# Gate, up and gated-unit projections: one 512-column matmul for the high weights in place of two of 256 columns

## The reference, cut to what matters

```
hidden = silu(h @ w_gate) * (h @ w_up)      # 11 chunks of 256 columns
x      = x + 0.5 * (hidden @ w_down)
```

## Time and profile before

| | |
|---|---|
| median of 3 runs | 1920.85 us (1920.28 to 1928.02) |
| the profiled execution's own time | 1923.98 us |
| its span, first to last instruction | 1922.2 us |
| mean granted TensorE clock | 0.972 of full speed |
| PE busy | 96% of the span |
| DVE busy | 43% |
| ACT busy | 34% |
| POOL busy | 9% |

### The profile page before, as it was taken

The page is one execution under the profiler, slowest core; times in us unless marked ns, Lnnn a source line. Parts: engine busy times, 40 slices in busy tenths (PEclk is TensorE's granted clock), DMA queues, the critical chain, the costliest instruction groups (busy, mean ns, idle before and its releaser), DMA issues.

```text
span 1922.2 us, 29735 instructions
## 1 busy us (share of the span) xinstructions
PE 1839.8 (96%) x12660; PEld 1520.6 (79%) x12660; DVE 835.5 (43%) x1028; ACT 652.4 (34%) x739; POOL 167.6 (9%) x83
## 2 busy tenths in 40 slices
PE   6997879999999998999999999999999999999998
PEld 4973744454554547999997999999999789999997
DVE  4325421111111107554576555565556445566544
ACT  3424210000000005434435543454435445354342
POOL 0110000000000000111000021112111000212110
PEclk8999879999999999999899999999999999999999
DMA  9329549999999995655543255555554545345550
GB/s 337 106 93 371 237 186 421 421 422 421 422 423 421 422 412 166 211 176 185 187 132 132 98 187 182 190 193 183 191 179 154 175 153 168 140 156 195 175 189 30
DMA packets 192020, 444.16 MB, mean 231 GB/s; under 512 B 9174, under 2 KB 140623, under 8 KB 164151
## 3 DMA queue, kind: packets, MB, share of 16 engines
q1 hardware_dynamic: 188736, 437.84, 61.7%
q10 hardware_dynamic: 2776, 2.90, 0.5%
q0 software_dynamic: 416, 2.09, 0.3%
HBM read 441.73 MB, written 1.06 MB: 230 GB/s over the span
## 4 chain that ended last, share of the span: by engine, by line
PE 92%; DVE 3%; ACT 2%; issue 1%; DMA 1%; ACTq 0%; POOL 0%; DVEq 0%
PE wk L1081 12%; PE wk L692 11%; PE wk L693 11%; PE wk L694 11%; PE acc L692 6%; PE acc L693 6%; PE acc L694 6%; PE wk L1101 6%; PE wk L1045 3%; PE acc L1061 3%; PE wk L742 2%; PE wk L743 2%; PE wk L745 1%; PE wk L770 1%; PE wk L778 1%
## 5 line engine op out<-in xcount | busy, mean ns | idle before, releaser
L522 DVE TENSOR_TENSOR w_lo<-ring,w_hi 128x2048 fp32r<-128x2048 f32 x197 | 452.0, 2297 | 391.9 <-ACT w_hi L513 391.8
L513 ACT ACTIVATE w_hi<-ring 128x2048 fp32r<-128x2048 f32 x198 | 377.4, 1907 | 510.5 <-PE wk L694 303.2
L692 PE MATMUL wk<-h_hi,w_hi 128*128 128x256 f32 x1752 | 499.0, 285 | 5.0 <-DVE h_lo L1951 5.0
L693 PE MATMUL wk<-h_lo,w_hi 128*128 128x256 f32 x1752 | 497.5, 284 | 0.0
L694 PE MATMUL wk<-h_hi,w_lo 128*128 128x256 f32 x1752 | 497.4, 284 | 0.0
L692 PEld LDWEIGHTS wk<-h_hi,w_hi 128*128 128x128 f32 x1752 | 338.2, 193 | 6.6 <-issue 6.5
L693 PEld LDWEIGHTS wk<-h_lo,w_hi 128*128 128x128 f32 x1752 | 338.1, 193 | 0.1
L694 PEld LDWEIGHTS wk<-h_hi,w_lo 128*128 128x128 f32 x1752 | 338.1, 193 | 0.0
L692 PE MATMUL acc<-hid_hi,w_hi 128*128 128x256 f32 x896 | 254.5, 284 | 2.7 <-POOL hid_lo L1838 2.7
L693 PE MATMUL acc<-hid_lo,w_hi 128*128 128x256 f32 x896 | 253.5, 283 | 0.0
L694 PE MATMUL acc<-hid_hi,w_lo 128*128 128x256 f32 x896 | 253.5, 283 | 0.0
(11 more groups left out here) (336 smaller groups left out, 2082.4 us busy)
## 6 DMA issues: line engine op xcount, KB each, us to landing
ring<-in_ffn_w_in_dram SPq DMA_DIRECT2D x88, 1024.0 KB, 5.1
ring<-in_w_gate_dram SPq DMA_DIRECT2D x64, 1024.0 KB, 13.7
ex_ring<-in_w_up_dram SPq DMA_DIRECT2D x64, 1024.0 KB, 17.0
ring<-in_ffn_w_out_dram SPq DMA_DIRECT2D x44, 1024.0 KB, 4.8
ex_ring<-in_w_down_dram SPq DMA_DIRECT2D x32, 1024.0 KB, 13.5
arena<-in_w_down_dram SPq DMA_DIRECT2D x32, 1024.0 KB, 12.6
ring<-in_w_ada_dram SPq DMA_DIRECT2D x24, 1024.0 KB, 7.8
ring<-in_b_w_in_dram SPq DMA_DIRECT2D x24, 1024.0 KB, 5.2
```

Source lines behind the costliest of these rows:

```text
L513: nc.scalar.activation(w_hi[:, v % SPLIT, 0:n], ring[:, u % RING, 0:n], ACT.Copy).then_inc(w_hi_ready, 1)
L522: eng.tensor_tensor(w_lo[:, v % SPLIT, 0:n], ring[:, u % RING, 0:n], w_hi[:, v % SPLIT, 0:n].bitcast(F32), ALU.subtract).then_inc(w_lo_rea ...
L692: mm(dst, w[0], x[0], start=first, stop=False, skip_group_check=True)
L693: mm(dst, w[0], x[1], start=False, stop=False, skip_group_check=True)
```

## The change

`h_hi` and `h_lo` become two halves of one tile `h_both`, so that one matmul can stream 256 high and 256 low columns (two runs, 2,048 elements apart). Its 512 results fill a whole bank: columns 0 to 255 hold high x high, columns 256 to 511 hold high x low, and a second matmul of 256 columns adds low weight x high activation to the latter. For each k-tile and m this is a 512-column and a 256-column matmul in place of three of 256 columns. The first gate unit of each layer keeps three matmuls of 256 columns (`first_halves_apart`).

A result takes two banks: gate always banks 0 and 1, up always 2 and 3, U units alternate between the pairs. The two column halves are added outside PE: ACT copies the low half to SBUF (`low_half`, `u_low_half`), DVE adds it to the high half (`summed`, and an add in `hidden` and in `scaled_u`), and then DVE does what it did before, from SBUF. The waits follow: gate and up of a chunk wait until the sums of the chunk before are made; a U unit waits for the sum two units earlier, and the first U unit for all results of the wide units. `totals` writes into an `acc` bank, and its wait is now ahead of the first down; `turn_wsp` writes into banks 0 and 1.

```diff
+        h_both = sb("h_both", [P, 2, KT, T], F32R)
+        h_hi, h_lo = h_both[:, 0, :, :], h_both[:, 1, :, :]
...
+            def halves_apart(banks, v):
+
+                wh, wl = halves(w_hi, v), halves(w_lo, v)
+                for m in range(2):
+                    f = slice(m * P, (m + 1) * P)
+                    for k in range(KT):
+                        mm(banks[:, m, :], wh[:, k, f], h_both[:, :, k, :], start=k == 0, stop=False,
+                           skip_group_check=True)
+                        last = mm(banks[:, m, T:2 * T], wl[:, k, f], h_hi[:, k, :], start=False, stop=k == KT - 1,
+                                  skip_group_check=True)
+                return last
...
 gate_up (PE)
-                            if i is not None:
-                                pe.wait_ge(hidden_ready, i * LOOP + (c0 + ch - 1))
...
-                        o = wk[:, 2 * (ch % 2) + j, :]
+                        if ch:
+                            n = c0 + ch
+                            pe.wait_ge((gate_summed, up_summed)[j], n if i is None else i * LOOP + n)
+                        banks = wk[:, 2 * j:2 * j + 2, :]
...
-                            last = project3(o, v)
+                            last = halves_apart(banks, v)
...
 U units (PE)
-            for a in range(12, 24):
-                v = split(U_B + a)
-                group(lambda b: project3(b, v), ends_unit=True)
+            pe.wait_ge(grp_out, g[0])
+            for a in range(12):
+                v = split(U_B + 12 + a)
+                if a >= 2:
+                    pe.wait_ge(u_summed, a - 1)
+                halves_apart(wk[:, 2 * (a % 2):2 * (a % 2) + 2, :], v).then_inc(unit_done, 1)
...
 swiglu (ACT)
+                    low_half(ch, i, 0)
                     split_high(v + SPLIT, i)
...
                     silu(ch, i)
+                    low_half(ch, i, 1)
                     split_high(v + 1 + SPLIT, i)
...
 swiglu (DVE), ahead of scaled, which now reads sil:
+                    dve.wait_ge(gate_copied, c0 + ch + 1 if i is None else i * LOOP + (c0 + ch + 1))
+                    V.tensor_tensor(sil[:, ch % 2, :, :], wk[:, 0:2, 0:T], gate_low, ALU.add).then_inc(gate_summed, 1)
...
 hidden (DVE)
+                    dve.wait_ge(up_copied, at(c0 + ch + 1))
+                    V.tensor_tensor(hid[:, ch % 2, :, :], wk[:, 2:4, 0:T], up_low, ALU.add).then_inc(up_summed, 1)
...
             for a in range(12):
+                u_low_half(a)
                 act.wait_ge(grp_out, 43 + 12 + a + 1)
...
 scaled_u (DVE)
+                dve.wait_ge(u_copied, a + 1)
+                b = wk[:, 2 * (a % 2):2 * (a % 2) + 2, :]
+                V.tensor_tensor(u_scaled_sb[:, a % 2, :, :], b[:, :, 0:T], u_low[:, a % 2, :, :], ALU.add).then_inc(u_summed, 1)
+                dve.wait_ge(u_summed, a + 1)
```

More of the change, by code:

```diff
@@ L283, in build @@
         sil_scaled = sem("sil_scaled")
+        gate_summed, up_summed, u_summed = sem("gate_summed"), sem("up_summed"), sem("u_summed")
+        gate_copied, up_copied, u_copied = sem("gate_copied"), sem("up_copied"), sem("u_copied")
         w_hi_ready, w_lo_ready, h_hi_ready, h_lo_ready = (sem("w_hi_ready"), sem("w_lo_ready"), sem("h_hi_ready"),
@@ L488, in build @@
         u_scaled_sb = nc.alloc_sbuf_tensor_at("u_scaled_sb", [P, 2, 2, T], F32, offset=hid_at)
+        u_low = nc.alloc_sbuf_tensor_at("u_low", [P, 2, 2, T], F32, offset=hid_at + 16 * T)
+        gate_low, up_low = (gated[:, 2048 + 512 * q:2560 + 512 * q].rearrange("p (m t) -> p m t", m=2) for q in range(2))
         def halves(hi, v, w=UW, rows=False):
@@ L712, in high_terms, with first_halves_apart @@
                 return mm(dst, w[1], x[0], start=False, stop=False, skip_group_check=True)
+            def halves_apart(banks, v):
[8 more added lines that the diff above has]
+                return last
+            def first_halves_apart(banks, v, fresh):
+                wh, wl = halves(w_hi, v), halves(w_lo, v)
+                for k in range(KT):
+                    pe.wait_ge(h_hi_ready, fresh + k + 1)
+                    for m in range(2):
+                        f = slice(m * P, (m + 1) * P)
+                        mm(banks[:, m, 0:T], wh[:, k, f], h_hi[:, k, :], start=k == 0, stop=False, skip_group_check=True)
+                        mm(banks[:, m, T:2 * T], wl[:, k, f], h_hi[:, k, :], start=False, stop=False,
+                           skip_group_check=True)
+                for k in range(KT):
+                    pe.wait_ge(h_lo_ready, fresh + k + 1)
+                    for m in range(2):
+                        last = mm(banks[:, m, T:2 * T], wh[:, k, m * P:(m + 1) * P], h_lo[:, k, :], start=False,
+                                  stop=k == KT - 1, skip_group_check=True)
+                return last
             def first_project3(dst, v, fresh):
@@ L1310, in turn_wsp @@
                 pe.wait_ge(wsp_masked, 1)
+                pe.wait_ge(gate_summed, C_F[2] + FFC)
                 for gr in range(BGROUPS):
-                    last = nc.tensor.transpose(wkf[:, 4 + gr // 2, (gr % 2) * P:(gr % 2 + 1) * P], wsp[:, gr, :], ident)
+                    last = nc.tensor.transpose(wkf[:, gr // 2, (gr % 2) * P:(gr % 2 + 1) * P], wsp[:, gr, :], ident)
                 last.then_inc(wsp_ps, 1)
@@ L1673, in high, with low_half @@
                     A(hid_hi[:, ch % 2, :, :], hid[:, ch % 2, :, :], ACT.Copy).then_inc(hid_hi_ready, 1)
+                def low_half(ch, i, up):
+                    n = c0 + ch
+                    u = gate_unit(u0, ch) + up
+                    act.wait_ge(unit_done, u + 1 if i is None else i * (3 * LOOP) + (u + 1))
+                    if ch:
+                        act.wait_ge((gate_summed, up_summed)[up], n if i is None else i * LOOP + n)
+                    A((gate_low, up_low)[up], wk[:, 2 * up:2 * up + 2, T:2 * T],
+                      ACT.Copy).then_inc((gate_copied, up_copied)[up], 1)
                 def step(ch, i):
                     v = v0 + (0 if ch == 0 else 3 * ch - 1)
+                    low_half(ch, i, 0)
                     split_high(v + SPLIT, i)
                     if ch == 0:
-                        fold_root(j_norm, wk[:, 3, :])
+                        fold_root(j_norm, accf[:, 0:512])
                     silu(ch, i)
+                    low_half(ch, i, 1)
                     split_high(v + 1 + SPLIT, i)
@@ L1770, in _ @@
             act.wait_ge(wsp_ps, 1)
-            A(wspT.rearrange("p g t -> p (g t)"), wk[:, 2:4, :].rearrange("p b n -> p (b n)"), ACT.Copy).then_inc(wsp_ready, 1)
+            A(wspT.rearrange("p g t -> p (g t)"), wk[:, 0:2, :].rearrange("p b n -> p (b n)"), ACT.Copy).then_inc(wsp_ready, 1)
             act.dma_start(binrow, b_b_in_2[:, BH:2 * BH]).then_inc(binrow_in, 16)
```

39 lines of the change are left out of this document (22 added, 17 removed).

## The result

The changed kernel takes 1926.18 us (median of 20 runs, 1924.17 to 1929.16), the kernel before beside it 1921.82 us (20 runs, 1918.21 to 1928.44). The ratio is 1.0019, with a 95% interval of 1.0010 to 1.0028: 1.9 to 5.4 us slower, 3.7 in the middle. That is inside the range and inside the 0.5% that was called no difference; but the sum had said -1.8 us, and the sign is wrong.

What follows compares the result with a forecast made beforehand. PE was taken to bound the kernel, on the chain for 92% of the span. Terms -17.6 + 3.9 + 0.2 + 1.2 + 10.5 gave -1.8 us, so 1919 us against 1920.85, range 1906 to 1933.

Steps and rivals of the forecast that it cites:

- the sum: Whole kernel: all terms added, -17.6 + 3.9 + 0.2 + 1.2 + 10.5 = -1.8 us.
- the term of the merged pairs: FFN gate and up units: 1,344 merged pairs save 13.1 ns each, -17.6 us.
- the fixed part stays: Rival, merged pairs: a matmul's cost beside its columns would not go away; 1937 us, chance 0.04.
- the assumption on the two runs: Merged pairs: a moving operand in two runs streams as fast as in one; rival of no gain 1937 us, 0.08.
- First chunk: First chunk of each layer: gate(1) waits for DVE's sum, 1.3 or 0.65 us by layer, +3.9 us.
- the +0.2 for the thin margin in FFN 0: FFN 0: gate(2)'s weights come only some 0.2 us early; +0.2 us, between 0 and 1.
- Last chunk: Last chunk of FFN 0 and 1: POOL's low part for down(10) comes 0.6 us later, +1.2 us.
- Even flow: FFN chunks 2 to 9: the new operations never make PE wait, cost 0, with some 6 us of cover.
- The stalling rival: FFN chunks: new waits cost 0.3 us in each of 44, 13 us, 1932 us; chance 0.05.
- U units: Block B's 12 U units: the add lengthens the DVE-ACT turn from 5.76 to 6.48 us; with the start +10.5 us.
- The rival of a hidden ring: U units: unseen slack hides the longer DVE-ACT turn, term -2.5 us, 1906 us; chance 0.12.
- The clock: Rival: idle PE ahead of L1359 lets half clock reach B's first down unit; up to 3.4 us, 1922 us, 0.10.

Runs made afterwards that it cites:

- contig: Changed kernel with high and low activations of one k-tile side by side, so the 512 columns are one run in memory: 1925.96 us, 1.0019.
- Twos: Changed kernel with two 512-column matmuls, then two of 256 columns, for each k-tile: 1920.67 us, 0.9989.
- grouped: Changed kernel with eight 512-column matmuls in a row, then eight of 256, for each half unit: 1919.41 us, 0.9988.
- all16: Changed kernel with all sixteen 512-column matmuls of a unit first, then all sixteen of 256: 1920.85 us, 0.9998.
- lag_unit: Changed kernel with each 256-column matmul one place later, behind the 512 of the next k: 1919.44 us, 0.9991.
- after_again: The changed kernel once more, unedited, for a second profile: 1926.17 us.
- u_only: Kernel before with only the 12 U units changed (merged matmuls, copies and adds), FFN as before: 1932.16 us, 1.0054.
- u_reorder: Changed kernel with ACT's split of the next weights ahead of gelu in the U units: 1909.13 us, 0.9940.
- before_again: The kernel before once more, unedited, for a second profile: 1924.07 us.
- experiment 6: Second profiles of the kernel before and of the changed kernel, both unedited: 1924.07 and 1926.17 us.
- u_old: Changed kernel with the 12 U units taken back to their old form, FFN still changed: 1911.50 us, 0.9946.
- skew: Changed kernel, widths still alternating, each 256-column matmul into the other bank than the 512 ahead of it: 1922.66 us, 1.0010.

## Why the prediction was right or wrong, step by step

**The step that failed: the term of the merged pairs, -17.6 us.** It was "1,344 x 13.1 ns", under the assumption that "a 512 between 256s keeps its pace; the wide units are the nearest rows". The wide units have only 512s behind 512s. Measured is 360.0 - 353.3 = 6.7 ns a pair, 1,344 x 6.7 = -9.0 us: 8.6 us missing, more than the whole miss of the sum (5.5). The mechanism, less fixed time with fewer matmuls, was right; its size was not. The rival that said so, "the fixed part stays" (0.04), came half true. contig shows that the assumption on the two runs held; it is the 512 between 256s that failed, by 236 ns in place of 226.9. Twos, grouped, all16 and lag_unit show that other orders of the same matmuls give back 3.5 to 5.4 ns of it. The unit is 5.66 us, not 5.55. By the formula of the Trainium skill (TensorE: Matmul & The Clock Gate, Back-to-back issue gap) the gain would be an estimated 2.5 ns; the measured 6.7 lies between it and the rows' 13.1, and agrees with neither.

**First chunk**: right in mechanism and nearly in size, 4.2 us in place of 3.9. From start to start, as the prediction reckons, FFN 2 has 1.29 for 1.3, FFN 1 and 3 have 0.49 for 0.65, and FFN 0, which was taken to look like FFN 2, has 1.96. The +0.2 for the thin margin in FFN 0 didn't come.

**Last chunk**: right, 0.46 us in FFN 0 and in FFN 1, 0.9 in place of 1.2. The high part starts 2.30 us behind the copy that marks the up unit's end (1263.72 to 1266.02), where it was 1.82 behind the split that marked it (1269.48 to 1271.30): 0.48 later, not 0.6, and 0.46 of that reaches down(10), so that "nothing is left over there" was right.

**Even flow**: right; PE busy for 130.00 of 130 us. The stalling rival is out.

**U units**: right. The turn was said to be 6.48 us and is 6.40 to 6.41; eleven carry 7.4, not 7.9. The start carries 2.9, not 2.65. Together, from the close of the rows to the spatial matmuls, it is +10.3 us by after_again (84.61 against 74.29), where U(0) has full clock, and +10.9 by the median of u_only, against 10.5. In the first profile it is +12.9, since the start then holds the low clock of U(0), which the prediction doesn't have. The rival of a hidden ring is out, and u_reorder shows the ring to be the cause: with one link taken out the turn falls to PE's unit, though every add and copy stays. One detail was wrong: PE waits 7.9 us ahead of L1394, not 12, because it had waited 4.1 us (0.43, 0.68, 0.51, 2.51) at U(8) to U(11) already.

**The clock**: partly came. The low stretch behind L1394 is there, and it reaches into the first down unit (0.77), but one like it lies behind L1359 in before_again, so no cost of the change is shown there. What the prediction missed is the other place, U(0), whose low clock costs 1.5 to 2.7 us in 11 of 13 profiles (experiment 6).

**The sum**: -9.0 + 4.2 + 0 + 0.9 + 10.3 = +6.4 us; measured +3.7 (1.9 to 5.4). The FFN layers as a whole are 4.9 us shorter in the traces and not 3.9 (in part for the chunks at the faster pace), which makes +5.4, or up to +8 with U(0) at low clock. So the stretches of the prediction explain the sign and more than the size; some 2 us or more are given back elsewhere, and where is not shown. The range and the chance of "same" were right because the terms of the U units and of the FFN nearly cancel in either case, which is in part luck: the largest term was off by half. The sign was wrong.

**What stays open**: the rule that picks one of the two paces; why kernels that differ little have mean clocks that differ by 0.003 (u_old and u_reorder high, all16 low), which is 5 us and more than most terms here; and the 2 us or so by which the measured change is smaller than its parts. In stretches that the change doesn't touch the time moves by some 3 us between two profiles of one kernel, which would cover that, but this is argued, not shown.

## What to carry to other kernels

Take the price of an instruction from rows where its neighbours are those that it will have: here a 512-column matmul cost 226.9 ns among its own kind and 236 between others. Read the cost of a wait from start to start: the idle time in brackets was 0.94 us where the unit came 1.29 us late. When work is moved onto engines that "have time", look for a ring among in-order engines (here scale, gelu, split, split) and add the new operation to its period: a ring that just fits under the bottleneck turns every added microsecond into one of the total, and moving one independent issue ahead of a wait can take the ring apart for more than the change itself is worth. Where a ratio is near 1, undo each half of the change by itself: here two effects of 10 us lay under 3.7.

## What was unexpected of the hardware

A stream of 512- and 256-column fp32r matmuls one by one has two steady paces, 353.3 and 346.8 ns a pair, at a granted clock of 1.00 in both; gate and up of the same kernel take 11.31 us in most chunks and 11.10 to 11.17 in a few, and in which ones differs from one execution to the next. In two orders (skew, lag_unit) the first unit of nearly every chunk ran at one and the second at the other; eleven U units in a row kept the faster in u_reorder, the slower in the changed kernel up to its first wait. And the low clock doesn't come with each execution at the same places: behind the same idle time of 1.54 us U(0) had 0.66 in one profile and 1.00 in the next.
